# Sliding-window attention with the turned probabilities split into two key blocks by VectorE, and the value rows as the stationary operand

## The reference, cut to what matters

```python
s = jnp.einsum('bnqhgd,bnkhd->bnhgqk', qb, kk) * (HEAD_DIM ** -0.5)   # kk: previous block and own block, 256 keys
band = (ki[None, :] <= qi[:, None]) & (qi[:, None] - ki[None, :] < WINDOW)
s = jnp.where(valid[None, :, None, None], s, -jnp.inf)
m = jnp.maximum(jnp.max(s, axis=-1, keepdims=True), sink)
p = jnp.exp(s - m)
p = p / (jnp.sum(p, axis=-1, keepdims=True) + jnp.exp(sink - m))
o = jnp.einsum('bnhgqk,bnkhd->bqnhgd', p, vv)
```

## Time and profile before

| what | value |
|---|---|
| median of 3 runs | 1230.08 us (1227.09 to 1230.37) |
| span of the profiled execution, first to last instruction | 1225.7 us |
| time of the profiled execution | not listed apart; the three runs lie 1.4 to 4.7 us above its span |
| PE busy | 1201.1 us, 98% |
| DVE, ACT, POOL busy | 876.6, 485.9, 229.2 us |
| attention on PE | first S at 46.94 us, last PV at 275.37 us |

### The profile page before, as it was taken

One profiled execution on the slowest core, in us unless ns is written; L12 is line 12 of the kernel. 1 busy time (PEld: TensorE's weight loads), 2 busy tenths in 40 slices (PEclk: granted clock), 3 DMA queues, 4 the chain that ended last, 5 costly groups with the idle time before them and its releaser, 6 DMA issues.

```text
span 1225.7 us, 23606 instructions
## 1 busy us (share of the span) xinstructions
PE 1201.1 (98%) x9397; PEld 1186.5 (97%) x9397; DVE 876.6 (72%) x1525; ACT 485.9 (40%) x997; POOL 229.2 (19%) x162
## 2 busy tenths in 40 slices
PE   9999999999999999998999999999999999999997
PEld 9899999999998999998999999999999999999996
DVE  4877566573747685789877888888888575567676
ACT  6643543625140364455422322222222335455542
POOL 1000010101010000000023255657664220000011
PEclk9999999999998999999999999999999999999999
DMA  9431100105264442234355465867675376686466
GB/s 305 107 91 36 36 19 1 37 18 88 37 106 69 106 160 83 70 96 130 87 163 162 160 208 188 265 218 241 203 246 187 125 230 203 201 256 190 142 154 118
DMA packets 174014, 169.82 MB, mean 139 GB/s; under 512 B 23144, under 2 KB 126328, under 8 KB 173376
## 3 DMA queue, kind: packets, MB, share of 16 engines
q1 hardware_dynamic: 171728, 164.78, 45.4%
q0 software_dynamic: 2176, 3.52, 1.8%
HBM read 116.73 MB, written 52.58 MB: 138 GB/s over the span
## 4 chain that ended last, share of the span: by engine, by line
PE 61%; DVE 5%; issue 1%; ACT 0%; DVEq 0%; ACTq 0%
PE pair L1808 33%; PE pair L1848 18%; PE pair L1767 6%; PE pair L1548 3%; DVE mix L2289 1%; DVE mix L2314 1%; DVE w_lo L2247 1%; DVE qinv L2285 1%; PE pair L1739 0%; PE pair L1680 0%; PE pair L1750 0%; DVE act_lo L2297 0%; DVE mix L2452 0%; DVE acc L2351 0%; DVE mix L2272 0%
## 5 line engine op out<-in xcount | busy, mean ns | idle before, releaser
L1808 PE MATMUL pair<-act_hi,w_hi 128*128 128x258 f32 x704 | 199.6, 284 | 4.3 <-DVE w_lo L2247 2.7
L1808 PE MATMUL pair<-act_hi,w_lo 128*128 128x258 f32 x704 | 198.9, 283 | 0.0
L1808 PE MATMUL pair<-act_lo,w_hi 128*128 128x258 f32 x704 | 198.7, 282 | 0.0
L1848 PE MATMUL pair<-a_ring,w_hi 128*128 128x258 f32 x1056 | 189.6, 283 | 0.6 <-DVE mix L2452 0.5
L1548 PE MATMUL pair<-act_hi,w_hi 128*128 128x344 f32 x528 | 177.8, 337 | 0.2 <-DVE w_lo L1921 0.2
L1548 PE MATMUL pair<-act_hi,w_lo 128*128 128x344 f32 x528 | 170.0, 322 | 0.0
L1548 PE MATMUL pair<-act_lo,w_hi 128*128 128x344 f32 x528 | 169.7, 321 | 0.0
L1848 PEld LDWEIGHTS pair<-a_ring,w_hi 128*128 128x128 f32 x1056 | 162.5, 189 | 1.6 <-DVE mix L2452 0.9
L1808 PE MATMUL pair<-s_hi,w_lo 128*128 128x258 f32 x528 | 149.3, 283 | 0.0
L1808 PE MATMUL pair<-s_hi,w_hi 128*128 128x258 f32 x528 | 149.2, 283 | 0.0
L1808 PE MATMUL pair<-mix_r,w_hi 128*128 128x258 f32 x528 | 149.0, 282 | 0.0
(11 more groups left out here) (323 smaller groups left out, 2639.3 us busy)
## 6 DMA issues: line engine op xcount, KB each, us to landing
raw<-w_up_dram SPq DMA_DIRECT2D x26, 512.0 KB, 5.1
a_in<-h_sums SPq DMA_DIRECT2D x44, 258.0 KB, 3.4
rawx<-w_gate_dram SPq DMA_DIRECT2D x22, 512.0 KB, 4.8
w_quarter<-w_down_dram SPq DMA_DIRECT2D x44, 256.0 KB, 3.9
w_sums<-w_quarter SPq DMA_DIRECT2D x44, 256.0 KB, 4.6
rawx<-w_sums SPq DMA_DIRECT2D x44, 256.0 KB, 3.8
raw<-w_in_dram SPq DMA_DIRECT2D x18, 512.0 KB, 4.4
h_scratch<-mix SPq DMA_DIRECT2D x23, 258.0 KB, 2.1
```

The source lines that it names most:

```text
L1808: mm = pe.matmul(pair[psum_pair(n)][:, s, 0:QW], a[:, r, half + k, :], b, start=(k == 0 and i == 0), stop=(k == 3 and i == 2))
L1848: mm = pe.matmul(dpair(mt)[:, s, 0:a.shape[1]], b[:, cut], a, start=(m == 0 and n == 0), stop=(m == HALVES - 1 and n == 2))
```

## The change

The two triangles of scores are put into one square before the maximum is taken. ACT copies the scores of the own block to `sm`; DVE overwrites the upper triangle with those of the block before (`copy_predicated` with the integer mask `tri`) and reduces to the maximum. The exponentials run over 128 keys for each group instead of 256. DVE now divides the probabilities by their sum in place (step N), before they are turned, so that nothing has to be scaled behind. PE turns one square for each group, two transposes instead of four. DVE reads them from PSUM, multiplies by the strict lower triangle of key over query to get the share of the block before (`pt_prev`) and subtracts it from the whole to get that of the own block (`pt_cur`). PE then takes the value rows as the stationary operand: two matmuls with 256 moving columns whose result is already turned, so the step OT is gone. ACT copies it to `mix` in two pieces.

```diff
     def attention_steps(tick):
         d = tick - AT0
-        out = []
         if d % 2 == 0:
-            for step, i in (("PT", d // 2 - 1), ("OT", d // 2 - 2), ("S", d // 2)):
+            steps = (("PV", d // 2 - 2), ("S", d // 2))
         else:
-            for step, i in (("PV", (d - 3) // 2), ("Q", (d + 1) // 2)):
+            steps = (("N", (d - 1) // 2), ("Q", (d + 1) // 2), ("PT", (d - 3) // 2))
...
 # ACT
                 elif step == "S":
+                    act.wait_ge(sem("at_s"), i + 1)
+                    if i >= 2:
+                        act.wait_ge(sem("at_exp"), i - 1)
+                    copy(sm[:, e], both_groups(BS)[:, :, WIN:]).then_inc(sem("at_sc"), 1)
                     act.wait_ge(sem("at_max"), i + 1)
...
-                elif step == "OT":
-                    act.wait_ge(sem("at_ot"), i + 1)
-                    copy(mix[:, t, P * j:P * j + P], BO[:, P:2 * P]).then_inc(sem("at_out"), 1)
+                elif step == "PV":
+                    act.wait_ge(sem("at_pv"), i + 1)
+                    for g in range(NKV):
+                        h = slice(HD * g, HD * g + HD)
+                        ins = copy(mix[h, t, P * j:P * j + P], BO[h, P * g:P * g + P])
+                    ins.then_inc(sem("at_out"), 1)
 # PE
                 elif step == "PT":
-                    pe.wait_ge(sem("at_exp"), i + 1)
+                    pe.wait_ge(sem("at_nrm"), i + 1)
...
                     for g in range(NKV):
-                        for kb in kbs:
-                            mm = pe.transpose(BP[:, P * (2 * g + kb):P * (2 * g + kb) + P], prob[:, g, P * kb:P * kb + P], ident[:])
+                        mm = pe.transpose(BP[:, P * g:P * g + P], prob[:, e, g, :], ident[:])
...
-                    for g in range(NKV):
-                        for kb in kbs:
-                            mm = pe.matmul(BO[:, HD * g:HD * g + HD], pt[:, 2 * g + kb, :], vrow[:, j - 1 + kb, HD * g:HD * g + HD],
-                                           start=(kb == kbs[0]), stop=(kb == 1))
+                    out = both_groups(BO[:, 0:NKV * P])
+                    mm = pe.matmul(out, vrow[:, j, :], pt_cur[:], start=True, stop=(j == 0))
+                    if j:
+                        mm = pe.matmul(out, vrow[:, j - 1, :], pt_prev[:], start=False, stop=True)
...
-                elif step == "OT":
-                    pe.wait_ge(sem("at_or"), i + 1)
-                    pe.transpose(BO[:, P:2 * P], orow[:].rearrange("p g d -> p (g d)"), ident[:]).then_inc(sem("at_ot"), 1)
 # DVE
                 elif step == "S":
-                    dve.wait_ge(sem("at_s"), i + 1)
...
+                    dve.wait_ge(sem("at_sc"), i + 1)
+                    mask = bc(tri[:, 0, :].bitcast(I32).unsqueeze(1), [P, NKV, WIN])
...
+                    then(dve.copy_predicated(sm[:, e], mask, other))
+                    then(dve.tensor_reduce(mx[:, e, :], sm[:, e], AX.X, ALU.max))
...
-                elif step == "PT":
+                elif step == "N":
+
                     dve.wait_ge(sem("at_exp"), i + 1)
                     then(dve.tensor_tensor(den[:, e, :], den[:, e, :], esk[:, e, :], ALU.add))
                     then(dve.reciprocal(rden[:, e, :], den[:, e, :]))
-                elif step == "PV":
-                    dve.wait_ge(sem("at_pv"), i + 1)
+                    for g in range(NKV):
+                        ins = dve.tensor_scalar(prob[:, e, g, :], prob[:, e, g, :], rden[:, e, g:g + 1], None, ALU.mult)
+                    ins.then_inc(sem("at_nrm"), 1)
+                elif step == "PT":
+
+                    dve.wait_ge(sem("at_pt"), i + 1)
...
+                        then(dve.tensor_tensor(pt_prev[:], turned, bc(tri[:, 1, :].unsqueeze(1), [P, NKV, P]), ALU.mult))
+                        dve.tensor_tensor(pt_cur[:], turned, pt_prev[:], ALU.subtract).then_inc(sem("at_ptc"), 1)
```

More of the change, by code:

```diff
@@ L10 @@
 U8 = mybir.dt.uint8
+I32 = mybir.dt.int32
 ALU = mybir.AluOpType
@@ L240, in build @@
     rstd = small("rstd", [P, RT])
-    orow = small("orow", [P, 2, HD])
+    neg = small("neg", [P, 1])
     ones = small("ones", [P, P])
@@ L282, in build @@
     at_att = o
-    sm, o = at("sm", [P, 2, 2 * WIN], F32, o)
-    prob, o = at("prob", [P, 2, 2 * WIN], F32, o)
-    pt, o = at("pt", [P, 4, P], F32, o)
-    amask, o = at("amask", [P, 2 * WIN], F32, o)
+    sm, o = at("sm", [P, 2, NKV, WIN], F32, o)
+    prob, o = at("prob", [P, 2, NKV, WIN], F32, o)
+    pt_cur, o = at("pt_cur", [P, NKV, P], F32, o)
+    pt_prev, o = at("pt_prev", [P, NKV, P], F32, o)
+    tri, o = at("tri", [P, 2, P], F32, o)
     at_hq = o
@@ L752, in _ @@
         load_rows(2)
-        for dst, src in ((amask[:], t_in["c_amask"]), (lmask32[:], t_in["c_lmask"]),
+        for dst, src in ((tri[:], t_in["c_tri"]), (lmask32[:], t_in["c_lmask"]),
                          (sink[:], t_in["attn_sinks"].partition_broadcast(P).rearrange("p o h -> p (o h)"))):
@@ L1614, in _ @@
                 t, j, e = i // NBLK, i % NBLK, i % 2
-                kbs = (1,) if j == 0 else (0, 1)
                 if step == "S":
@@ L2113, in _ @@
                     then(dve.reciprocal(rden[:, e, :], den[:, e, :]))
-                elif step == "PV":
-                    dve.wait_ge(sem("at_pv"), i + 1)
-                    if i:
-                        dve.wait_ge(sem("at_ot"), i)
-                    dve.tensor_tensor(orow[:], BO[:, 0:P].rearrange("p (g d) -> p g d", g=2),
-                                      bc(rden[:, e, :].unsqueeze(2), [P, 2, HD]), ALU.mult).then_inc(sem("at_or"), 1)
+                    for g in range(NKV):
[3 more added lines that the diff above has]
+                    dve.wait_ge(sem("at_pt"), i + 1)
+                    if i:
+                        dve.wait_ge(sem("at_pv"), i)
+                    turned = both_groups(BP[:, 0:NKV * P])
+                    if j:
+                        then(dve.tensor_tensor(pt_prev[:], turned, bc(tri[:, 1, :].unsqueeze(1), [P, NKV, P]), ALU.mult))
+                        dve.tensor_tensor(pt_cur[:], turned, pt_prev[:], ALU.subtract).then_inc(sem("at_ptc"), 1)
+                    else:
+                        dve.tensor_copy(pt_cur[:], turned).then_inc(sem("at_ptc"), 1)
             if tick % 2 == 0 and 0 < tick // 2 <= UNITS - CH:
```

41 lines of the change are left out of this document (14 added, 27 removed).

## The result

The changed kernel takes **1261.1 us** (median of 4 runs, 1259.2 to 1263.6), the one before 1228.6 on the same chip: the ratio is 1.0261, with a 95% interval of 1.0241 to 1.0281. It is slower by 2.6%, where 1.1% were forecast, and 1261 lies above the range of 1232 to 1256. The profiled span is 1259.0 us against 1225.7.

The account below looks back on a forecast made before the run. PE, 98% busy, would wait in a ring through ACT and DVE; +15.3 - 4.5 + 0.5 + 1.5 = +12.8 us on 1230.1 gives 1243 us, 1.1% slower, range 1232 to 1256.

Parts of the forecast that it names:

- the ring: Items 1 to 19: PE's values wait for `pt_cur` through DVE and ACT; 6.6 us a turn, +15.3 us for the stretch.
- the prices: New DVE instructions: predicated copy and maximum 0.42 us each (bounds 0.29 to 1.30, 0.28 to 0.57); values' products on PE 0.87.
- rival (b): PE's 256-column values' products as fast as the bound below, 0.46 us less every turn and item; 1228 us, 10%.
- PE's gain: Transposes leaving PE: 88 at 0.11 us, 9.7 us in all, 0.33 for an item with j > 0.
- The rest: From item 19 on, intervals mostly above the ring, so PE keeps 12 x 0.33 = 4.0 us, plus 0.5 at both ends: -4.5.
- the recurrence's ticks 0.3 us shorter: Sign expected in the changed kernel's profile: ticks with recurrence steps, from item 19 on, 0.3 us shorter.
- +0.5: From item 19 on, DVE's 1.1 us more per item makes it a little late in one or two ticks: +0.5 us.
- the clock, +1.5: One short stretch at the low clock, with the longest wait expected at `lower_bound`, about 2.5 to 3 us: +1.5 us.
- Rival (c): Waits at weight and rope items lower the clock more than once, three to six stretches, +6 to +12 us: 1249 to 1255; 24%.

Follow-up runs that it names:

- e1: The changed kernel with DVE doing the parting (split of the turned probabilities) first, ahead of the division N and the queries' split; 1244.5 us, ratio 1.0118.
- the fourth: The changed kernel without the division of the probabilities by their sum (two scalings left out on DVE); 1252.0 us, ratio 1.0178.
- e2: The changed kernel with PE doing the scores ahead of the values' products, and ACT copying those out behind its copy of the scores; 1251.2 us, ratio 1.0174.
- e12: e9's order on DVE, e7's elsewhere, with ACT rounding the next item's `q_hi` between the copy of the scores and the wait for the maximum; 1225.5 us.
- e6: e1 with DVE doing a head's normalization of the recurrence one tick later, behind the attention steps; 1244.7 us, ratio 1.0123.
- e7: e5 and e6 together, with ACT making the recurrence's key rows between the copy of the scores and the exponentials; 1235.4 us, ratio 1.0054.
- e10: The changed kernel, ring kept, with only ACT's key rows moved ahead of the exponentials and DVE's head normalization one tick later; 1258.8 us, ratio 1.0240.
- e5: e1 with PE doing the values' products one tick later, behind an odd tick's products; 1241.6 us, ratio 1.0101.
- e11: Control: the kernel before the change with the moves of e9, as far as it has the steps; 1225.8 us, ratio 0.9978.
- e9: e7 with `q_hi` ahead of ACT's weight tile, `q_lo` ahead of DVE's parting and N, and the lower bounds' second half after them; 1246.9 us.

## Why the prediction was right and wrong

**Right: the ring.** Place, members and size were right. A turn measured 6.56 for 6.62; the stretch of items 1 to 19 took 123.7 for 121.6, +17.4 for the forecast +15.3. On PE two errors cancel: behind a wait the values took 0.78 and the scores 1.05 (149.41 to 150.19 to 151.24), for 0.87 and 0.95. The first experiment opened the ring with one edit, and the fourth showed that DVE's part counts one for one. What the prediction did not see is a second loop just below it, DVE and ACT alone, 6.11 us in an item with a rope unit; it came to light in e2.

**Right: the prices.** All new DVE instructions lie at the value taken, not at a bound. Groups by line and shape in the changed kernel, with the mean in ns:

```profile
L2101 DVE TENSOR_REDUCE mx<-sm 128x2 f32<-128x256 f32 x32 | 13.4, 420 | 1.1
L2100 DVE COPY_PREDICATED sm<-tri,pair 128x256 f32<-128x256 int32 x28 | 12.5, 446 | 32.2 <-ACT sm L1100 32.2
```

The predicated copy of 256 elements with long runs takes 446 ns, far from the bound of 1.30 us; the 724 and 1299 of the earlier trace rows are for 512 elements. The values' products cost as forecast: in e12 their records are 0.217 us apart (128.81 - 128.38 = 0.43 for two). So rival (b) does not hold. The rule of the Trainium skill (TensorE: Matmul & The Clock Gate, section "Back-to-back issue gap"), taken as the prediction took it, with one gap for each record, would have them 0.109 apart by estimate, and this trace does not agree for fp32.

**Right: PE's gain.** 0.33 us an item was forecast. Where PE does not wait, a plain item takes 5.56 in e1 and in e12 for 5.91: 0.35.

**Wrong: "The rest", -4.5.** The step read: "From item 19 on an interval lasts 6.2 to 10.4 us, mostly above the ring with its recurrence steps: there PE keeps its gain". Measured were +13.0 in that stretch. I compared the length of PE's interval with the length of the ring as if the ring stayed 6.6 us long. But the recurrence's steps stand in the same queues on ACT and DVE, between the members of the ring. Its normalization (1.29 us, and 4.71 of waiting for ACT ahead of it) is in front of N, the queries and the parting; ACT's key rows are behind the exponentials, and so, by 1.07 us, are its squares. The prediction's own sign for this step, the recurrence's ticks 0.3 us shorter, did not appear: tick 70 was 5.3 longer and tick 73 1.6. I had seen that DVE has more work there and priced it at +0.5, as work; what counted was what is queued behind a wait. e6 shows it for tick 70 (8.00 to 4.35), and e7 for the stretch, at 101.9 us. e10 shows that the two causes don't add: with the ring left in, moving those steps gave 5.2 us in the stretch and next to nothing in the time (2.3, within the intervals); with the parting first and the values later (e5 to e7) it gave 7.5 and 6.2.

**Wrong in size and place: the clock, +1.5.** I counted one short low stretch in items 1 to 19, where the longest wait was expected. That wait came (2.41 us, behind `lower_bound`), but no low stretch: the granted clock was 1.00 with 19.6 us of PE's time not busy. The low stretches came in items 19 to 31, as shown above, for an estimated 4 us. Behind item 31 the clock gives and takes. Ticks 95 and 96 hold the same work in both kernels, 5.71 and 3.45 us before and 6.94 and 5.03 now, with two low stretches: +2.8. Ticks 112 to 116 took 26.86 us before, with the low stretch of the earlier trace rows, and 25.48 now, with a shorter one: -1.4. In the kernel before, and in the changed one:

```profile
391.80:401.90 10.10, 9.91 (x46) 9.54 (x47) 5.42 (x10) 0.49 (x1) 0.00 (x0) 0.51 0.36 104
```

```profile
428.60:435.20 6.60, 6.60 (x35) 6.11 (x34) 3.62 (x7) 0.49 (x1) 1.22 (x1) 0.50 0.62 163
```

So the clock's share is some 5 us (4 + 2.8 - 1.4, an estimate) for 1.5. Rival (c) had it falling more than once, at 1249 to 1255, but put it down to the weight and rope items.

**The sum by its terms:** ring +17.4 (+15.3); items 19 to 31 with their own low clock +13.0 (-4.5 and +0.5); behind them +3.1, in which the clock has +2.8 and -1.4 and the rest are differences of about 1 us and less (the forecast of +1.5 was for a low stretch that did not come); together +33.5, less 0.1 at the start, for the measured +33.3 of the spans.

**Open.** Whether the change is worth anything once both kernels have their best order (e11 and e12 overlap). Why the part behind item 31 varies from 962.5 to 971.1 us over these profiles, though the change leaves its work alone: the low clock is one part of it, and in e12 waits for `w_lo` of the feed-forward part are another (4.9 us for 2.7), but no experiment took either alone. Nor did one take the clock's 4 us in items 19 to 31 apart from the waits; in e7 both are gone.

## What to carry to other kernels

When a change makes an engine's wait part of a ring, list everything that stands in the queues between its members, from other stages too: a step that is harmless behind the ring costs its whole length, and its own wait, once it is in front of a member. Look for the loops that need fewer engines too: e2 cut the ring on PE and was left with DVE's own, and the parting paid off only inside a wait that DVE has anyway (e1). A ring's length holds only for ticks that carry nothing else. Before moving a step to the front of a queue, ask on which engine its input is made and behind what (e9 closed a new ring of 6.31 us); put it into a wait that the engine has anyway (e12, behind the copy of the scores), and move all that the ring touches together, since one at a time only shows the next wait.

## What the runs showed of the hardware

The same short wait does and does not go before a low clock. In the kernel before and in the changed one PE waits 0.69 us for DVE's `hk` ahead of the same level products, as the rows from each show:

```profile
316.70 1.95 PE L1680 MATMUL pair<-hq,hk 128*124 128x64 f32 x16 [0.69 <-DVE hk L2063]
```

```profile
347.45 1.95 PE L1672 MATMUL pair<-hq,hk 128*124 128x64 f32 x16 [0.69 <-DVE hk L2056]
```

Behind it the kernel before stays at 1.00 (2.4 GHz), and the changed one has two stretches at 0.50 (1.2 GHz), apart from each other by one at full clock. Busy times by stretch, from 2.55 us behind the start of these products on, PE first and the clock before the last two columns, of the one and of the other:

```profile
319.25:329.45 10.20, 10.15 (x81) 9.86 (x79) 7.02 (x15) 1.44 (x2) 0.12 (x1) 1.00 0.06 16
```

```profile
350.00:353.40 3.40, 3.40 (x15) 3.40 (x14) 2.09 (x4) 0.00 (x0) 0.00 (x0) 0.50 0.15 42
353.40:356.70 3.30, 3.30 (x31) 3.30 (x31) 1.74 (x3) 0.00 (x0) 0.00 (x0) 1.00 0.00 0
356.80:360.20 3.40, 3.40 (x15) 3.40 (x14) 1.64 (x6) 1.44 (x2) 0.00 (x0) 0.50 0.02 5
```

At the low level PE got through 15 matmuls in 3.4 us, at the high one through 31 in 3.3, so such a stretch costs half its length in work. And the changed kernel's first stretch, in which PE stands idle for a sixth of the time in 18 waits of 0.26 to 2.41 us, kept the full clock throughout. The longest of them is as long as the 2.31 us that a low stretch followed in the earlier trace rows:

```profile
88.21 0.70 PE L1635 MATMUL pair<-pt_cur,vrow 128*128 128x256 f32 x2 [2.41 <-DVE pt_cur L2122]
```

What makes the difference between these places was not settled.
